# Dilated attention's distances added in VectorE's reads of the scores, with three smaller moves ahead of it

## The reference

```python
bias = -slopes[:, None, None] * dist          # dist = dilation * |rel|, slopes[h] = 2 ** -(h + 1)
s = jnp.einsum('bnqche,bnkche->bnchqk', qs, kw).astype(jnp.float32) * scale + bias
s = jnp.where(mask, s, MASK_VALUE)
m = jnp.max(s, axis=-1, keepdims=True)
e = jnp.exp(s - m)
l = jnp.sum(e, axis=-1, keepdims=True)
o = jnp.einsum('bnchqk,bnkche->bnqche', e.astype(v.dtype), vw)
```

## Time and profile before

| | |
|---|---|
| median of 3 runs | 2908.43 us (2906.88 to 2909.33) |
| the profiled execution's own time | 2905.6 us |
| its span in the trace | 2903.6 us |
| mean granted TensorE clock | 0.974 |
| busy: PE, PEld | 2727.3 us (94%), 2256.5 us (78%) |
| busy: DVE, ACT, POOL | 2044.4 (70%), 1556.1 (54%), 1053.2 us (36%) |

### The profile page before, as it was taken

One profiled execution on the slowest core, in us unless ns is written; L12 is line 12 of the kernel. 1 busy time (PEld: TensorE's weight loads), 2 busy tenths in 40 slices (PEclk: granted clock), 3 DMA queues, 4 the chain that ended last, 5 costly groups with the idle time before them and its releaser, 6 DMA issues. The chain is left out here.

```text
span 2903.6 us, 54522 instructions
## 1 busy us (share of the span) xinstructions
PE 2727.3 (94%) x21026; PEld 2256.5 (78%) x21026; DVE 2044.4 (70%) x3027; ACT 1556.1 (54%) x3111; POOL 1053.2 (36%) x803
## 2 busy tenths in 40 slices
PE   7899989999799999989999899899899999899998
PEld 5678867888599999978887678688677778777776
DVE  5767687666799999967777766433567777566775
ACT  5575455644588888867776212322343343455553
POOL 4667656777222223129550544200021111311211
PEclk9999999999899999999999899899999999899999
DMA  3432323332411120123443757242165466644441
GB/s 116 131 109 88 101 77 94 106 109 88 126 39 42 44 54 25 26 58 119 119 119 101 248 200 263 92 141 76 57 174 131 115 161 178 175 137 138 149 152 68
DMA packets 317295, 330.12 MB, mean 114 GB/s; under 512 B 24385, under 2 KB 259953, under 8 KB 313841
## 3 DMA queue, kind: packets, MB, share of 16 engines
q1 hardware_dynamic: 287184, 292.85, 33.1%
q0 software_dynamic: 6912, 23.07, 2.7%
q10 hardware_dynamic: 22944, 10.76, 1.6%
HBM read 217.13 MB, written 109.47 MB: 112 GB/s over the span
## 5 line engine op out<-in xcount | busy, mean ns | idle before, releaser
L1049 PE MATMUL p_acc<-p_y_hi,p_x_hi 128*128 128x512 f32 x904 | 363.2, 402 | 11.4 <-DVE p_y_lo L841 3.8
L1049 PE MATMUL p_acc<-p_y_lo,p_x_hi 128*128 128x512 f32 x904 | 357.4, 395 | 0.0
L1049 PE MATMUL p_acc<-p_y_hi,p_x_lo 128*128 128x512 f32 x904 | 357.0, 395 | 0.0
L562 POOL TENSOR_TENSOR p_x_lo<-k_carry,p_x_hi 128x1024 fp32r<-128x1024 f32 x113 | 281.0, 2493 | 133.8 <-ACT p_x_hi L634 133.8
L2080 PEld LDWEIGHTS d_out<-d_v,d_w_t 64*128 64x128 f32 x4096 | 261.7, 188 | 15.6 <-ACT d_a_parts L1928 13.2
L2080 PE MATMUL d_out<-d_v,d_w_t 64*128 64x128 f32 x4096 | 268.4, 274 | 1.2 <-ACT d_a_parts L1928 1.2
L1913 ACT ACTIVATE d_e<-d_e,d_neg_top 128x2048 f32<-128x2048 f32 x128 | 257.1, 2008 | 20.1 <-DVE d_neg_top L1993 20.1
L920 DVE RECIPROCAL p_aux<-p_aux 128x512 f32<-128x512 f32 x64 | 215.1, 3361 | 56.1 <-ACT p_aux L730 56.1
L1584 PE MATMUL s_acc<-h_y_hi,s_x_hi 128*128 128x512 f32 x560 | 224.1, 400 | 24.0 <-DVE s_x_lo L1388 13.7
L1584 PE MATMUL s_acc<-h_y_hi,s_x_lo 128*128 128x512 f32 x560 | 220.7, 394 | 0.0
L1584 PE MATMUL s_acc<-h_y_lo,s_x_hi 128*128 128x512 f32 x560 | 220.6, 394 | 0.0
(11 more groups left out here) (372 smaller groups left out, 7148.8 us busy)
## 6 DMA issues: line engine op xcount, KB each, us to landing
k_carry<-in_w_in SPq DMA_DIRECT2D x128, 256.0 KB, 3.2
k_carry<-in_a_w_in POOLq DMA_DIRECT2D x72, 256.0 KB, 3.6
cols<-p_z SPq DMA_DIRECT2D x64, 256.0 KB, 2.5
o_parts<-l_stage SPq DMA_DIRECT2D x192, 66.0 KB, 1.7
m_o<-o_parts SPq DMA_DIRECT2D x48, 264.0 KB, 5.9
k_carry<-cols SPq DMA_DIRECT2D x48, 256.0 KB, 4.7
j_x_second<-x SPq DMA_DIRECT2D x20, 512.0 KB, 3.7
k_carry<-x SPq DMA_DIRECT2D x20, 512.0 KB, 3.6
```

The source lines that it names most:

```text
L562: pool.tensor_tensor(x_lo[:, m % RING], inputs.place(x_place(m)), x_hi[:, m % RING].bitcast(F32), ALU.subtract).then_inc(x_lo_made, 1)
L1049: mm = pe.matmul(bank_of(n, j), x_part[:, n % RING, j, kt], y_part[:, y_slot(n), kt], start=(kt == 0 and m == 0 and not (g == 0 and n % 2 ...
```

## The change

1. **Dilated stage.** The bias matmuls go. Tables of plain distances times the dilation (128x256, by level and by place at an edge or between) lie in SBUF; DVE reads each head's scores with them in one instruction that adds, takes the extremum and writes the sum to `l_e`: four instructions per step where one reduction was. The exponentials read and write `l_e` in place, with scale -1; each waits for its own maximum. `copy_out` moves from DVE to ACT, behind `move(n, 0)`. PE's `scores` waits for DVE's reads of two steps before, and runs its passes unit by unit. The gains of the dilated q take the heads' slopes in (8 small instructions in the projection). POOL fills the tables in 3 pieces where it had 8.
2. **First loads.** k goes to `k_carry[:, 4:6]`, q to `[:, 6:8]`, and SP issues them in four pieces behind the first four products of the last pair, where they stood together near the end. The dilated stage's raw q and k take the lower half, and the merge's weights swap halves in turn.
3. **First splits.** ACT and DVE make only the first 128 queries' q and half-width pieces of k; POOL makes the rest of the first q, and holds `q_lo` of the second block until the first unit is mixed. The distances are folded in three pieces.
4. **End of the projection.** `sum_squares` of the last product stands ahead of `turn_rows`, and `sqrt` ahead of `keep_rows`.

```diff
+                if g == PAIRS_IN_ALL - 1 and form < 4:
+                    sp.wait_ge(acc_full, 2 * n)
+                    if form == 0:
+                        sp.wait_ge(y_lo_made, 22)
+                        wait_all_stored(sp, 2 * QUAD_OUT * (PAIRS_IN_ALL - 2))
...
-                if n == PRODUCTS - 3:
-                    sp.wait_ge(x_lo_made, PRODUCTS)
-                    sp.wait_ge(y_lo_made, 22)
-                    wait_all_stored(sp, 2 * QUAD_OUT * (PAIRS_IN_ALL - 1))
...
-            for n in (PRODUCTS - 2, PRODUCTS - 1):
-                if row_at(n) is not None:
-                    keep_rows(n)
+            if row_at(PRODUCTS - 2) is not None:
+                keep_rows(PRODUCTS - 2)
             if norm_at(PRODUCTS - 1) is not None:
                 sqrt(PRODUCTS - 1)
+            if row_at(PRODUCTS - 1) is not None:
+                keep_rows(PRODUCTS - 1)
...
+            if norm_at(PRODUCTS - 1) is not None:
+                sum_squares(PRODUCTS - 1)
             if row_at(PRODUCTS - 1) is not None:
                 turn_rows(PRODUCTS - 1, 1)
-            if norm_at(PRODUCTS - 1) is not None:
-                sum_squares(PRODUCTS - 1)
 
...
+        self.k_raw = carry[:, 4:6]
+        self.q_raw = carry[:, 6:8].rearrange("p a (b n) -> p a b n", b=2)
...
+        self.tables = ph.sb("tables", [P, 2, 3, 2 * P])
+        self.own = ph.sb("own", [P, P])
+        self.near = ph.sb("near", [P, 2, 2 * P])
+        self.raw = carry[:, 0:4].rearrange("p (a b) n -> p a (b n)", a=2)
...
+        near, away = self.near[:, 0], self.near[:, 1]
+        pool.iota(away, pattern=[[-1, 2 * P]], base=REACH, channel_multiplier=1,
                   allow_small_or_imprecise_dtypes=True).then_inc(self.counted, 1)
-
-    def fold_distance(self, dve):
-
-        dve.wait_ge(self.counted, 1)
-        dve.scalar_tensor_tensor(out=self.near[:, 0], in0=self.near[:, 1], scalar=-1.0, in1=self.near[:, 1],
-                                 op0=ALU.mult, op1=ALU.min).then_inc(self.counted, 1)
-
-    def fill(self, pool, ident, piece):
-
-        near, tables, own, slopes = self.near[:, 0], self.tables, self.own, self.slopes
...
+        near = self.near[:, 0]
         if piece == 0:
+            pool.wait_ge(self.counted, 4)
+            for n, (base, step, channel) in enumerate(((2 * REACH, -1, 1), (0, 1, -1))):
+                pool.affine_select(out=near, in_=near, compare_op=ALU.is_ge, fill=-MASKED, base=base,
+                                   pattern=[[step, 2 * P]], channel_multiplier=channel).then_inc(self.counted, 1)
+                pool.wait_ge(self.counted, 5 + n)
         elif piece == 1:
+            for level in range(2):
+                for place in range(3):
+                    pool.tensor_scalar(self.tables[:, level, place], near, float(DILATIONS[level]), None, ALU.mult)\
+                        .then_inc(self.made, 1)
         else:
+            pool.tensor_scalar(self.own[:, :], near[:, REACH:REACH + P], float(DILATIONS[2]), None, ALU.mult).then_inc(self.made, 1)
+            pool.wait_ge(self.made, 7)
+            pool.memset(self.tables[:, :, 0, 0:REACH], -MASKED).then_inc(self.made, 1)
+            pool.memset(self.tables[:, :, 2, 2 * P - REACH:2 * P], -MASKED).then_inc(self.made, 1)
+
+    def wait_made(self, eng):
+
+        eng.wait_ge(self.made, 9)
...
             if h == 0:
-                eng.wait_ge(k_first_made, s + 1)
+                eng.wait_ge(k_first_made, 2 * s + half + 1)
+        FOLDS = ((NEAR, NEAR + HALF), (NEAR + HALF, SPAN), (0, NEAR))
...
+            make_q_hi(0, slice(P, QUAD))
+            make_q_lo(0, slice(P, QUAD))
             bias.count_off(pool)
             make_q_hi(1)
+            pool.wait_ge(mixed, 1)
             make_q_lo(1)
...
-            act.activation(q_hi[:, 0], q_raw[:, 0], ACT.Copy).then_inc(q_first_hi, 1)
-            def fold(n, first, last):
+            act.activation(q_hi[:, 0, :, 0:P], q_raw[:, 0, :, 0:P], ACT.Copy).then_inc(q_first_hi, 1)
+
+            def make_first_k_hi(s, half):
+                keys = slice(half * BANK, (half + 1) * BANK)
+                act.activation(k_hi[:, 0, s, keys], k_raw[:, s, keys], ACT.Copy).then_inc(k_first_hi, 1)
+
+            def fold(n):
+                first, last = FOLDS[n]
                 act.wait_ge(counted, n + 1)
                 counts = e[:, 2].rearrange("p b n -> p (b n)")[:, first:last]
                 act.activation(dist[:, first:last], counts, ACT.Abs).then_inc(dist_made, 1)
 
             act.wait_ge(k_loaded, 64)
-            for s in range(2):
-                act.activation(k_hi[:, 0, s], k_raw[:, s], ACT.Copy).then_inc(k_first_hi, 1)
-            fold(0, NEAR, SPAN)
-            fold(1, 0, NEAR)
+            make_first_k_hi(0, 0)
+            make_first_k_hi(0, 1)
+            make_first_k_hi(1, 0)
+            fold(0)
+            fold(1)
+            make_first_k_hi(1, 1)
+            fold(2)
...
-            dve.tensor_tensor(q_lo[:, 0], q_raw[:, 0], q_hi[:, 0].bitcast(F32), ALU.subtract).then_inc(q_first_made, 1)
-            for s in range(2):
-                dve.wait_ge(k_first_hi, s + 1)
-                dve.tensor_tensor(k_lo[:, 0, s], k_raw[:, s], k_hi[:, 0, s].bitcast(F32), ALU.subtract)\
+            dve.tensor_tensor(q_lo[:, 0, :, 0:P], q_raw[:, 0, :, 0:P], q_hi[:, 0, :, 0:P].bitcast(F32), ALU.subtract)\
+               .then_inc(q_first_made, 1)
+
+            def make_first_k_lo(s, half):
+                keys = slice(half * BANK, (half + 1) * BANK)
+                dve.wait_ge(k_first_hi, 2 * s + half + 1)
+                dve.tensor_tensor(k_lo[:, 0, s, keys], k_raw[:, s, keys], k_hi[:, 0, s, keys].bitcast(F32), ALU.subtract)\
                    .then_inc(k_first_made, 1)
+
+            make_first_k_lo(0, 0)
+            make_first_k_lo(0, 1)
+            make_first_k_lo(1, 0)
             dve.wait_ge(dist_made, 1)
...
+                if m == -2:
+                    dve.wait_ge(dist_made, 2)
                 if m + 2 < UNITS:
                     bias_and_top(m + 2, 0, 1)
+                if m == -2:
+                    make_first_k_lo(1, 1)
+                if m + 2 < UNITS:
...
-                    bias.fold_distance(dve)
-                    dve.wait_ge(dist_made, 2)
+                    dve.wait_ge(dist_made, 3)
...
 
-    def bias_of(n, own, half):
-
-        d, _, b, _ = step_of(n)[0]
+    def bias_of(n, j):
+
+        d, _, b, _ = step_of(n)[j]
         if d == NT:
-            return bias.own[own, half].rearrange("p a n -> p (a n)")
-        first = 0 if b == 0 else 2 if b == NT // d - 2 else 1
-        return bias.tables[own, half, first:first + 2].rearrange("p a n -> p (a n)")
+            return bias.own[:, :]
+        return bias.tables[:, level_of(n), 0 if b == 0 else 2 if b == NT // d - 1 else 1]
...
-                act.wait_ge(top_made, n + 1)
-                if n >= 2:
-                    act.wait_ge(turned, n - 1)
                 for h in range(2):
-                    act.activation(e[:, u % 4, h, 0:width(n)], score[:, 2 * (n % 2) + h, scores_of(n, j)], ACT.Exp,
-                                   bias=stage[:, u % SLOTS, 2 * HD + h:2 * HD + h + 1],
+                    own = e[:, u % 4, h, 0:width(n)]
+                    act.wait_ge(top_made, 2 * u + h + 1)
+                    act.activation(own, own, ACT.Exp, bias=stage[:, u % SLOTS, 2 * HD + h:2 * HD + h + 1], scale=-1.0,
                                    accum_out=stage[:, u % SLOTS, 2 * HD + 2 + h:2 * HD + 3 + h]).then_inc(exped, 1)
...
+            def copy_out(n):
+                act.wait_ge(valued, n + 1)
+                if n >= 2:
+                    act.wait_ge(o_turned, n - 1)
+                act.activation(o_t[:, n % 2].rearrange("p u n -> p (u n)"), out[:, 0, 0:2 * P], ACT.Copy).then_inc(o_copied, 1)
...
-            for n in range(TOTAL):
+            for n in range(TOTAL + 1):
                 if n + 1 < TOTAL:
                     exp(2 * n + 2)
                     exp(2 * n + 3)
-                move(n, 0)
+                if n < TOTAL:
+                    move(n, 0)
+                if n >= 1:
+                    copy_out(n - 1)
...
             def top(n):
+                pair, level = n // SPP, level_of(n)
                 dve.wait_ge(scored, n + 1)
-                for u in (2 * n, 2 * n + 1):
+                for j in range(2):
+                    u = 2 * n + j
                     if u >= SLOTS:
                         dve.wait_ge(stored[u % SLOTS], 16 * (u // SLOTS))
-                own = score[:, 2 * (n % 2):2 * (n % 2) + 2]
-                if width(n) == P:
-                    own = own.rearrange("p h (b n) -> p b h n", n=P)[:, 0:4:3]
-                else:
-                    own = own.rearrange("p h (u n) -> p u h n", u=2)
-                dve.tensor_reduce(stage[:, 2 * n % SLOTS:2 * n % SLOTS + 2, 2 * HD:2 * HD + 2], own, AX_X, ALU.max, negate=True)\
-                   .then_inc(top_made, 1)
+                    for h in range(2):
```

(21 more changed lines are left out.)

136 lines of the change are left out of this document (55 added, 81 removed).

## The result

| | before | changed |
|---|---|---|
| median of 4 runs each | 2907.65 us (2902.72 to 2909.33) | 2869.23 us (2867.97 to 2873.46) |
| the profiled execution, its span | 2905.6, 2903.6 us | 2868.9, 2867.1 us |
| busy PE, DVE, ACT, POOL | 2727.3, 2044.4, 1556.1, 1053.2 us | 2688.6, 2032.5, 1593.3, 1049.9 us |
| mean granted clock | 0.974 | 0.974 |

The ratio is 0.9873, 95% interval 0.9856 to 0.989. Four more runs of the changed kernel gave 2873.42 us (ratio 0.9888, 0.9873 to 0.9903); over all eight its median is 2872.2 us.

What follows compares the result with a forecast made beforehand. The prediction took PE to bound the dilated stage, and after the change a chain of waits between engines. From 2905.6 us it took 35.5, 2.7 and 1.6, giving 2865.8 for the profiled execution and 2868.5 for the median; range 2856 to 2885 us.

Steps and rivals of the forecast that it cites:

- The bias on PE: Dilated stage: taking out the bias matmuls shortens PE's round by 0.50 us a step, to 2.77 us wide and 2.07 narrow.
- DVE, four reads 0.41 us apart: Dilated stage: four reads make 1.64 us, DVE's round 2.57 us, below PE's; spacing taken from the window attention.
- ACT, 0.49 us from one exponential to the next, 2.74 a round: Dilated stage: with `copy_out` and exponentials from SBUF, ACT's round is 2.74 us wide, 2.09 narrow, within 0.03 of PE's.
- The chain, 5.78 us for two steps: Dilated stage: waits through `move`, transposes, scores, `values`, `copy_out` and exponentials span two steps, giving 2.89 us wide, 2.22 narrow.
- 64 x 0.38 and 32 x 0.35, 35.5 us: Dilated stage's whole gain: 64 wide steps from 3.27 to 2.89 us, 32 narrow ones from 2.57 to 2.22.
- End of the projection, 2.7 us: Projection's end: with `sum_squares` and the square root earlier, the last reciprocal and what follows come 2.7 us sooner.
- SP's earlier loads cost nothing.: Projection's end: the earlier loads are eight issues behind finished products, and later stores wait for later events; 0 us.
- Start of the differential stage, 1.6 us: Differential stage's start: smaller first splits bring the first read forward, and the time stays gained as PE is busy; 1.6 us.
- The chain holds less, PE the bound: Dilated stage: the chain falls below 5.54 us and PE's 2.77 and 2.07 us rule; 2856 us, chance 0.20.
- ACT bound outright: Dilated stage: exponential and readback don't overlap, ACT's round is 3.14 us wide, 2.49 narrow; 2893 us, chance 0.08.
- DVE bound: Dilated stage: longer reads make DVE the bound and the kernel slower; 2930 us at 0.70 us per read, chance 0.02.
- bias of no use: Dilated stage: PE would wait for DVE's reads where it now multiplies; time stays near 2905 us, chance 0.03.

Runs made afterwards that it cites:

- bias_products_kept: Changed kernel with four more products of the old bias products' size ahead of each step's scores, which overwrite them: 2900.95 us, ratio to before 0.9983.
- three experiments: Changed kernel, separately: `copy_out` back on DVE, 2860.87 us; `copy_out` on ACT a step later between exponentials, 2862.0; PE's `values` ahead of `turn_out`, 2858.68.
- the second profile: The changed kernel run and profiled once more, nothing changed: 2873.42 us, ratio to before 0.9888, dilated stage 267.67 us.
- squares_late: Changed kernel with `turn_rows` again ahead of the last `sum_squares` and `sqrt` behind `keep_rows`: 2875.59 us, ratio to before 0.9892.
- loads_late: Changed kernel with SP's first loads of the differential stage again in one block near the projection's end: 2873.5 us, ratio to before 0.9878.
- values_first: Changed kernel with PE's `values` of step n-1 ahead of `turn_out` of step n-2: 2858.68 us, ratio to before 0.9833.

## Why the prediction was right, and where it was off

The forecast was 2868.5 us, the first four runs gave 2869.23, all eight 2872.2. Term by term:

**The bias on PE, 0.50 us a step (0.44 to 0.55).** Right. 3.27 - 2.80 = 0.47 wide and 2.57 - 2.11 = 0.46 narrow, from the kernels in which PE is the bound again, and `bias_products_kept` puts back exactly that. The low end of the range took 0.15 us for a drain, and no row shows so much. The score matmuls ahead of the 1403.61 of the earlier trace rows read

```profile
1403.04 0.41 PE L2447 MATMUL l_score<-l_k_lo,l_q_hi 64*128 64x256 f32 x4
1403.28 0.40 PE L2447 MATMUL l_score<-l_k_hi,l_q_lo 64*128 64x256 f32 x4
```

Four start in 0.24 us, and `turn_out` 0.33 us after the last four began, so 0.09 is left over; two thirds of 0.81 - 0.09 are 0.48, which is what came.

**DVE, four reads 0.41 us apart.** Too dear: 0.421 us long and 0.345 apart. The row in the window attention was not of its own kind: there the bound of the minimum is read from a tensor, here it is a constant. The profile's groups have both forms side by side in the differential stage, 1285 ns with a tensor (`d_half_top`) and 1223 without, in this kernel:

```profile
L2013 DVE CUSTOM_DVE_ANT_0 d_e<-d_score,d_dist,d_half_top 128x1024 f32<-128x1024 f32 x128 | 164.5, 1285 | 7.2 <-PE d_score L2078 0.9
...
L2013 DVE CUSTOM_DVE_ANT_0 d_e<-d_score,d_dist 128x1024 f32<-128x1024 f32 x128 | 156.5, 1223 | 16.3 <-PE d_score L2078 16.2
```

That is 62 ns; at 256 columns it is 481 ns in the window attention against 421 here, 60 ns, the size of the error. No run changes the bound alone, so the cause is argued from these groups. It changed no sum, since DVE wasn't the bound.

**ACT, 0.49 us from one exponential to the next, 2.74 a round.** Right: 1325.51 to 1326.00, and 499 ns long against 473 from PSUM. The Trainium skill's page "VectorE: DVE Perf Modes", section on the TRN2 errata, makes the difference between the two sources 52 cycles, 43 ns. The prediction's "the trace agrees" goes too far. The traces show it in direction but 26 ns in size at 256 columns (499 to 473) and 25 at 128 (391 to 366), 10 us over the 384 exponentials and not 17; and none of it was on the path once the chain was gone.

**The chain, 5.78 us for two steps, 2.89 wide and 2.22 narrow.** The mechanism is right, and it is what three experiments take away. Measured it is 5.84: 0.67 from `move` to transposes (0.65 forecast), 0.50 to the first score (0.52), 1.28 to `values` (1.23), 1.14 to `copy_out` (1.14), 0.29 (0.28), and 1.96 for the exponentials (1.96). Steps are 2.925 and 2.26 us. Evenly spaced steps came only in part of the last pair; elsewhere it is 2.81 and 3.04 in turn, where only every second step waits, by 0.2 us, and the mean is what two steps of the chain give.

**64 x 0.38 and 32 x 0.35, 35.5 us.** This is the term that was mis-sized: 29.2 us, 30.2 in the second profile. By the steps of one pair of heads above, 73.01 - 65.62 = 7.39 us against 8.88. Of the 1.49 missing, 0.68 are in the fifteen wide steps (43.98 us against 15 x 2.89 = 43.35, and one of them 0.25 longer than its like), 0.21 in the six narrow ones, and 0.60 in the three steps at the seams between wide and narrow: they took 2.84, 3.01 and 2.72 before and 2.72, 2.55 and 2.82 now, so 0.48 us in place of 3 x 0.36. The prediction priced all 96 steps as if each were in the middle of its level. The last seam, from narrow to wide, is the one that got longer: there PE waits for ACT's four wide exponentials, in each of the three places where a pair follows another:

```profile
1486.46 0.71 PE L2479 MATMUL l_turn<-k_ident,l_e 64*128 64x64 f32 x16 [0.64 <-ACT l_e L2373]
```

The four pairs gained 6.5, 7.4, 6.9 and 6.9 us (the last over 23 steps). In the first the second step took 3.84 us (before 3.10), across the stretch in which the clock was granted at 0.50. In the third one step took 3.76 us from `turn_out` to `turn_out` in place of about 2.8: PE stood 0.5 us in the midst of its transposes with nothing named that it waited for (at 1453.36). What held it there stays open. Another 1.4 us were gained ahead of the first transposes, which come 4.40 us after the first score and came 5.79 before.

**End of the projection, 2.7 us (2.0 to 2.7).** 2.85, by `squares_late`.

**"SP's earlier loads cost nothing."** The step of the prediction that failed, to the good: they gave 1.0 us (`loads_late`), and 1.9 if the 0.86 us that no undo gave back are theirs too, which its place in the same wait suggests and no run shows. The prediction looked at what the moved loads wait for, and not at what they had been running beside: the stores for which DVE waited 3.31 us.

**Start of the differential stage, 1.6 us (0 to 1.9).** 0.8. The first read did come 1.8 us nearer, as said. "From there PE is busy, so the time stays gained" is what failed: the next link was the first exponential, and ahead of it stood ACT's fold and 1.28 us of table load, 0.35 us from being the last.

**The rivals.** The chain holds less, PE the bound (2856 us): not here, but it is what the three chain edits make of the kernel, at 2858.7 to 2862.0 us. ACT bound outright, DVE bound, bias of no use: none; PE never waited for the reads in the 240 us of the window. The waits were named right (ACT's `move` and exponentials, 9.5 us over some 86 steps, 0.11 each against 0.12, the 0.5 us at 1453.36 among them). The sign "a granted clock below 1.00" did show in the stage's first 10 us, in both kernels, and not after.

The forecast's sum for the profiled execution, 2865.8 us, is nearer to its 2868.9 than its terms deserve: 6.3 us too much for the dilated stage, 0.8 for the differential start and 3.2 lost in the second projection stood against 2.1 too little in the tail and the 4.5 us before it, and neither the 3.2 nor the 4.5 is the change's.

## What to carry to other kernels

When work is taken from the bounding engine and the others come near it, sum each engine's round, and then follow the chain of waits round the loop over as many steps as it spans: here two steps took 5.84 us where PE's rounds took 5.60, and moving one small copy, or swapping two groups on PE, was worth 11 to 14 us of the stage. Price an instruction by a row of its own kind down to the operands, price the steps at the seams by themselves, and ask of every moved transfer what it had been running beside.

## What the runs showed that was not expected

**The order in which two engines start goes with 3.4 us.** The 4.5 us ahead of the projection's last block come mostly from here: PE's matmuls in the kernel before run 1.0 us behind those of the changed kernel's first profile at 390 us, and 4.4 at 444. The kernel before, timeline at 417 us, POOL's subtractions and DVE's addition:

```profile
417.12 6.62 POOL L562 TENSOR_TENSOR p_x_lo<-k_carry,p_x_hi 128x1024 fp32r<-128x1024 f32 x2 [1.19 <-ACT p_x_hi L634]
```
```profile
418.00 3.45 DVE L836 TENSOR_TENSOR k_carry<-k_carry 128x1024 f32<-128x1024 f32 x1
```

and the changed kernel in its first profile:

```profile
417.39 5.12 POOL L563 TENSOR_TENSOR p_x_lo<-k_carry,p_x_hi 128x1024 fp32r<-128x1024 f32 x2 [2.83 <-ACT p_x_hi L635]
```
```profile
416.63 1.21 DVE L838 TENSOR_TENSOR k_carry<-k_carry 128x1024 f32<-128x1024 f32 x1
```

Where DVE's addition starts inside POOL's pair it takes 3.45 us, and POOL's pair 6.62; where it starts 0.8 us ahead of POOL it takes 1.21, and POOL's pair 5.12. Of the twelve traces, the two that reach the last block at 736 us (`values_first` is the other) show 1.21, and the ten at 739 to 741 us show 3.44 to 3.46. What makes DVE come first was not followed further, and no edit set the order.

**A DVE read whose bound comes from a tensor is about 60 ns longer**, at 1024 columns (1285 to 1223) as at 256 (0.48 us in the earlier trace rows, 0.421 here). No run varied this alone.
